# A hybrid encoder layer on one core: outputs of attention and of the delta rule handed on in fp32, split by the merge, and the first delta tile joined from 16-row blocks

## What is computed

```
ya = oa.reshape(b, t, WIDTH_A) @ w['w_branch_a']      # oa: attention over the selected keys
yb = ob @ w['w_branch_b']                             # ob: gated delta rule, normed and gated
merged = jax.nn.sigmoid(gate_a) * ya + jax.nn.sigmoid(gate_b) * yb
x = x + merged @ w['w_out']
```

```
sol = lax.linalg.triangular_solve(a, rhs, left_side=True, lower=True, unit_diagonal=True)
v_new = u - w @ state
new_state = state * exp(g_last) + k_faded @ v_new
```

## Time and profile before

| | us |
|---|---|
| median of three runs (lowest, highest) | 3028.71 (3026.67, 3028.89) |
| the profiled execution, its own time | 3023.2 |
| its span in the profile | 3021.4 |
| attend ends, first DMA of delta | 1702.39 |
| first DMA of merge | 1940.39 |
| first product with w_out in merge | 1990.40 |

### The profile page before, as it was taken

One profiled execution on the slowest core, in us unless ns is written; L12 is line 12 of the kernel. 1 busy time (PEld: TensorE's weight loads), 2 busy tenths in 40 slices (PEclk: granted clock), 3 DMA queues, 4 the chain that ended last, 5 costly groups with the idle time before them and its releaser, 6 DMA issues. The chain is left out here.

```text
span 3021.4 us, 43869 instructions
## 1 busy us (share of the span) xinstructions
PE 2860.3 (95%) x16073; PEld 2681.7 (89%) x16073; DVE 1655.0 (55%) x2958; ACT 848.2 (28%) x1485; POOL 373.0 (12%) x470
## 2 busy tenths in 40 slices
PE   6999999999989999999889788699899999999998
PEld 6999999999989789999878688588789999999997
DVE  5444444444451378899355467467744444444445
ACT  4111111111132434554276334211221111111112
POOL 0000000000000034444230266210000000000000
PEclk9999999999999999999989799899999999999999
DMA  4111111111022112222210323732121111111111
GB/s 135 53 43 42 42 42 42 42 42 42 8 53 47 29 53 89 82 89 89 75 53 20 88 68 98 222 124 82 42 64 42 42 42 42 42 42 42 42 35 63
DMA packets 248861, 183.55 MB, mean 61 GB/s; under 512 B 46329, under 2 KB 230185, under 8 KB 248754
## 3 DMA queue, kind: packets, MB, share of 16 engines
q1 hardware_dynamic: 241602, 153.74, 17.6%
q10 hardware_dynamic: 4752, 18.94, 1.7%
q0 software_dynamic: 2400, 9.44, 0.9%
HBM read 142.37 MB, written 39.65 MB: 60 GB/s over the span
## 5 line engine op out<-in xcount | busy, mean ns | idle before, releaser
L506 DVE TENSOR_TENSOR ffn_prod<-ffn_silu,ffn_p_up 128x384 f32<-128x384 f32 x132 | 73.2, 554 | 768.7 <-ACT ffn_silu L426 768.7
L488 DVE SCALAR_TENSOR_TENSOR x<-ffn_p_down,x 128x512 f32<-128x512 f32 x738 | 474.9, 687 | 1.3 <-PE ffn_p_down L157 1.3
L157 PE MATMUL ffn_p_gate<-ffn_hT_hi,ffn_g_hi 128*128 128x384 f32 x1056 | 356.7, 338 | 17.9 <-ACT ffn_silu L426 10.8
L157 PE MATMUL ffn_p_gate<-ffn_hT_lo,ffn_g_hi 128*128 128x384 f32 x1056 | 355.3, 336 | 0.0
L157 PE MATMUL ffn_p_gate<-ffn_hT_hi,ffn_g_lo 128*128 128x384 f32 x1056 | 355.1, 336 | 0.0
L157 PE MATMUL ffn_p_up<-ffn_hT_hi,ffn_u_hi 128*128 128x384 f32 x1056 | 353.8, 335 | 0.0
L157 PE MATMUL ffn_p_up<-ffn_hT_hi,ffn_u_lo 128*128 128x384 f32 x1056 | 353.2, 334 | 0.0
L157 PE MATMUL ffn_p_up<-ffn_hT_lo,ffn_u_hi 128*128 128x384 f32 x1056 | 353.0, 334 | 0.0
L426 ACT ACTIVATE ffn_silu<-ffn_p_gate 128x384 f32<-128x384 f32 x132 | 64.9, 492 | 870.5 <-PE ffn_p_up L157 870.4
L157 PE MATMUL ffn_p_down<-o_c_hi,o_t_lo 128*128 128x512 f32 x756 | 295.4, 391 | 0.0
L157 PE MATMUL ffn_p_down<-o_c_lo,o_t_hi 128*128 128x512 f32 x756 | 295.0, 390 | 0.0
(11 more groups left out here) (390 smaller groups left out, 5137.8 us busy)
## 6 DMA issues: line engine op xcount, KB each, us to landing
ffn_raw_g<-in_ffn_w_gate SPq DMA_DIRECT2D x44, 512.0 KB, 5.1
ffn_raw_u<-in_ffn_w_up SPq DMA_DIRECT2D x44, 512.0 KB, 6.2
ffn_raw_d<-in_ffn_w_down SPq DMA_DIRECT2D x44, 512.0 KB, 3.6
h_raw<-in_w_in SPq DMA_DIRECT2D x32, 512.0 KB, 3.9
projected_d<-sp_stage ACTq DMA_DIRECT2D x20, 576.0 KB, 2.8
conv_d<-sp_stage ACTq DMA_DIRECT2D x12, 576.0 KB, 3.2
dl_qkv<-conv_d SPq DMA_DIRECT2D x27, 256.0 KB, 4.1
x<-in_x_prompt SPq DMA_DIRECT2D x8, 512.0 KB, 8.3
```

Of the source, the lines that this page charges most:

```text
L157: mm = nc.tensor.matmul(out, stationary(k)[a], moving(k)[b], start=(start and at == 0 and i == 0), stop=(stop and 3 * at + i == n - 1))
L488: nc.vector.scalar_tensor_tensor(out=xs, in0=p_down[(NO * q + o) % 4][:], scalar=0.5, in1=xs, op0=ALU.mult, op1=ALU.add).then_inc(added, 1)
L506: nc.vector.tensor_tensor(prod[:, slot], silu[:, slot], p_up[slot][:, 0:TG], ALU.mult).then_inc(prod_done, 1)
```

## The change

Three things. (1) `attend` writes its turned output once, unsplit, from two alternating buffers (`oT[:, t % 2]`), and the sample units once, from a buffer of their own; DVE's `keep_rest` and `keep_rest_dec` go, `turn_out_dec` follows three units behind instead of four. (2) `delta` writes the gated output unsplit and straight from the gate's buffer, for tiles 3 to 8; tiles 0 to 2 (the merge's first third) are split by `keep_high` and `keep_rest` into SBUF operands that stay there. The attended output of the first third is loaded raw at step 5 and split in step 7. A gate buffer of tile 5 or later is reloaded only when the store out of it has landed, and the stage's end waits for those stores. The merge loads raw thirds, casts on ACT and subtracts on DVE, with one raw buffer for a and, for b, the second half of `gate_a` and part of `gate_b`'s; the third third is loaded when the second has been split. (3) Tile 0 is solved on POOL like the others, so its step has three levels; fronts of tiles 0 and 1 are both made ahead of step 0. `take_log` moves ahead of `keep_high`, `sum_squares` of the last two tiles ahead of the state products of the sample tile, and the constant planes shrink from ten to three.

```diff
@@ attend @@
-            for t in range(NTP):
-                sp.wait_ge(oT_rest, t + 1)
-                for i in range(2):
-                    sp.dma_start(a_parts_d[i][...], oT[:, i].bitcast(F32)).then_inc(stored, 16)
+            for t in range(NTP):
+                sp.wait_ge(oT_ready, t + 1)
+                sp.dma_start(attended_d[...], oT[:, t % 2]).then_inc(stored[t % 2], 16)
+            sp.wait_ge(oT_ready, NTP + 2)
+            sp.dma_start(attended_d[...], oT_dec[:]).then_inc(stored_dec, 16)
...
@@ delta, SP @@
             def load_gate(n):
-                if n >= 2:
+                if 2 <= n < 2 + FIRST:
                     sp.wait_ge(lo_done, n - 1)
+                elif n >= 2:
+                    sp.wait_ge(gated_stored, 16 * (n - 1 - FIRST))
...
             def store(n):
-                sp.wait_ge(lo_done, n + 1)
-                for i in range(2):
-                    sp.dma_start(b_parts_d[i][...], parts[:, i].bitcast(F32)).then_inc(parts_stored, 16)
+                sp.wait_ge(normed, n + 1)
+                sp.dma_start(gated_d[...], gate[:, n % 2]).then_inc(gated_stored, 16)
...
             load(2)
-            to_blocks(1)
             sp.dma_start(gain[:], ...)
             load_gate(0)
             load_gate(1)
+            send_lower(0)
+            to_blocks(0)
+            send_lower(1)
+            from_blocks(0)
+            to_blocks(1)
             for n in range(NT):
...
                 if n + 1 < NT:
                     from_blocks(n + 1)
                 if n + 2 < NT:
+                    send_lower(n + 2)
                     to_blocks(n + 2)
+                if n >= 3 + FIRST:
+                    store(n - 3)
                 if n >= 3:
-                    store(n - 3)
                     load_gate(n - 1)
-                if n == NTP - 2:
-                    first.load(sp, a_parts_d, b_parts_d)
+                if n == NTP - 3:
+                    first.load(sp, attended_d)
...
+            sp.wait_ge(gated_stored, 16 * (NT - FIRST))
@@ delta, PE @@
-            rows_and_k(0)
-            q_and_v(0)
-            turn_hats(0)
-            grams_k(0)
-            grams_q(0)
-            turn_first()
+            for m in range(2):
+                rows_and_k(m)
+                q_and_v(m)
+                turn_hats(m)
+                grams_k(m)
+                grams_q(m)
@@ delta, ACT and DVE @@
-                    if n >= 3 and third == 2:
-                        keep_high(n - 3)
+                    if n == NTP - 1 and third == 0:
+                        first.keep_high_a(act)
                     if n >= 2 and third == 2:
                         take_log(n - 2)
+                    if 3 <= n < 3 + FIRST and third == 2:
+                        keep_high(n - 3)
...
+                    elif n == NTP - 1 and third == 0:
+                        first.keep_rest_a(dve)
...
-                if n >= 3:
-                    keep_rest(n - 3)
+                    if 3 <= n < 3 + FIRST and third == 2:
+                        keep_rest(n - 3)
@@ delta, POOL @@
             front(0)
-            for m in range(1, NT):
+            front(1)
+            solve(0)
+            solve(1)
+            for m in range(2, NT):
                 front(m)
                 solve(m)
@@ merge @@
+            for g in range(1, NG):
+                if g >= 2:
+                    sp.wait_ge(a_rest, g - 1)
+                sp.dma_start(raw_a[:], attended_d[...]).then_inc(raw_a_in, 16)
+                if g >= 2:
+                    sp.wait_ge(b_rest, 2 * (g - 1))
+                for i in range(2):
+                    sp.dma_start(raw_b[i], gated_d[...]).then_inc(raw_b_in, 16)
             weights.load_out(sp, 0)
             weights.load_branches(sp, 1)
...
             weights.branches_hi(act, 0)
-            weights.out_hi(act, 0)
-            weights.branches_hi(act, 1)
             for n in range(KD):
                 for g in range(NG):
+                    if n == 0 and g + 1 < NG:
+                        split_high(g + 1)
+                    if n == 0 and g == 1:
+                        weights.out_hi(act, 0)
+                        weights.branches_hi(act, 1)
                     act.wait_ge(summed, NG * n + g + 1)
...
+                    if n == 0 and g + 1 < NG:
+                        split_rest(g + 1)
...
+                    if n == 0 and g:
+                        pe.wait_ge(a_rest, g)
...
+                    if n == 0 and g:
+                        pe.wait_ge(b_rest, 2 * g)
```

More of the change, by code:

```diff
@@ L2134, in _ @@
             for h in range(HB):
+                if h < 2:
+                    sum_squares(NTP - 1 + h)
                 pe.wait_ge(v_spread, h + 1)
@@ L2264, in keep_rest @@
                 dve.wait_ge(hi_done, n + 1)
[L2265 to L2268 removed]
+                tokens = slice(n * P, (n + 1) * P)
+                nc.vector.tensor_tensor(first.b_lo[:, :, tokens], gate[:, n % 2], first.b_hi[:, :, tokens].bitcast(F32),
+                                        ALU.subtract).then_inc(lo_done, 1)
             def next_state(n):
@@ L2436, in keep_high @@
                 act.wait_ge(normed, n + 1)
-                if n:
-                    act.wait_ge(parts_stored, 32 * n)
-                nc.scalar.copy(parts[:, 0], gate[:, n % 2]).then_inc(hi_done, 1)
+                nc.scalar.copy(first.b_hi[:, :, n * P:(n + 1) * P], gate[:, n % 2]).then_inc(hi_done, 1)
             def step(n):
@@ L2628, in __init__, with load, keep_high_a, keep_rest_a @@
     def __init__(self, nc, s):
-        self.parts = [[s.sbuf(f"{n}_{part}", [P, HB, TG], F32R) for part in ("hi", "lo")] for n in ("a", "b")]
-        self.outputs = s.sbuf("outputs", [P, 2, HB, P], F32R)
-        self.operands_in, self.parts_stored = s.sem("operands_in"), s.sem("parts_stored")
-    def load(self, sp, *parts_d):
-        sp.wait_ge(self.parts_stored, 32 * (TG // P))
-        load_operands(sp, self.parts, parts_d, slice(0, TG), self.operands_in)
-def load_operands(sp, parts, parts_d, tokens, landed):
-    for part, part_d in zip(parts, parts_d):
-        for i in range(2):
-            sp.dma_start(part[i][:].bitcast(F32), part_d[i][:, :, tokens].rearrange("n p t -> p n t")).then_inc(landed, 16)
-def merge(nc, x, weights, ops, first, parts_d, projected_d):
+        self.nc = nc
+        self.a_hi, self.a_lo, self.b_hi, self.b_lo = (s.sbuf(n, [P, HB, TG], F32R) for n in ("a_hi", "a_lo", "b_hi", "b_lo"))
+        self.raw = s.sbuf("raw", [P, HB, TG])
+        self.raw_in, self.high, self.rest = s.sem("raw_in"), s.sem("high"), s.sem("rest")
+    def load(self, sp, attended_d):
+        sp.dma_start(self.raw[:], attended_d[:, :, 0:TG].rearrange("n p t -> p n t")).then_inc(self.raw_in, 16)
+    def keep_high_a(self, act):
+        act.wait_ge(self.raw_in, 16)
+        self.nc.scalar.copy(self.a_hi[:], self.raw[:]).then_inc(self.high, 1)
+    def keep_rest_a(self, dve):
+        dve.wait_ge(self.high, 1)
+        self.nc.vector.tensor_tensor(self.a_lo[:], self.raw[:], self.a_hi[:].bitcast(F32), ALU.subtract).then_inc(self.rest, 1)
+def merge(nc, x, weights, ops, first, attended_d, gated_d, projected_d):
     KB = HB
```

315 lines of the change are left out of this document (126 added, 189 removed).

## The result

Five executions of the changed kernel took 3003.05 to 3013.57 us, median 3009.31; five of the kernel before 3024.92 to 3028.89, median 3026.67. The ratio is 0.9941, with a 95% interval of 0.9926 to 0.9955: faster by 17.4 us, half as much again as the 11.8 forecast, and inside the range by 1.3 us at its lower end (3008). The profiled execution, 3003.05, is the quickest of the five, so its profile shows 20.1 less than that of before, not 17.4. "Delta" is from its first DMA to the merge's first DMA, "merge's start" from there to the first product with `w_out`.

A forecast was written before the change was run, and what follows sets the result against it. PE bounds the untouched feed-forward stages; attend's end, delta (solve loop first, then DVE and PE handing over) and the merge's first 50 us can move. -2.4 + 4.7 - 3.0 - 4.3 - 6.8 = -11.8, so 3016.9 us; range 3008 to 3026.

The forecast's parts named there:

- Attend, -2.4: End of attend: last units no longer wait for high part, rest and store in turn; -2.4 us, bounds -0.6 to -3.4.
- Delta's start, +4.7: Start of delta: solve 1 starts 5.9 us later, 1.2 won back; +4.7, bounds +3.5 and +7.5.
- the solve's loop: In delta: solve, writes, packed reads, next solve; a period of 20.2 us, to which the steps may shrink.
- Delta's steps, -3.0: Steps of delta: earlier `take_log` -1.9, two rests gone -1.3 and -0.7, step 7's added work +0.9; -3.0 us, bounds -5 and 0.
- 0.48 a step: Steps 3 to 6 of delta: PE's wait that goes with `take_log` ahead of `keep_high`; -1.9 us in all.
- the 3.6 of the estimate: Step 7 of delta: the 128x1536 subtraction beside solve 8 grows from 1.85 to 3.6 us, making the steps' sum 1.8 worse.
- Delta's end, -4.3: End of delta: last store follows the norm -4.2, its landing +2.3, one store less -0.4, earlier norm -2.0; bounds -6 and -1.
- one of the signs of being wrong: Tail of delta: the prediction is wrong if gate loads stall POOL there.
- Merge, -6.8: Start of the merge: cast of `w_out` at 18.4 us against 25.3, so `out` starts 6.8 sooner; bounds -9.5 and +4.5.
- delta's solves don't bind all the way: Rival in delta: nine solves stay the bound, start costs 7.5, steps give nothing; -6.0 us, 3022.7; 15%.
- a third's round of load and split in the merge: Rival: if it takes over 12 us rather than 8, the merge gains nothing; -5.0 us, 3023.7; 15%.
- solve 0 was not late: Rival in delta: solve 0 starts only at 1739.5, start costs 20.2, steps give nothing; +6.7 us, 3035.4; 6%.

The follow-up runs named there:

- again: The changed kernel once more, unchanged, timed and profiled a second time: 3007.21 us, 0.9936 of the kernel before.
- six_levels: The changed kernel without its third part: tile 0 joined from 2-row blocks in six levels again, not solved on POOL; 3003.78 us, 0.9926 of the kernel before.
- all_rests: The changed kernel with cast and subtraction also for tiles 3 and 4, in steps 6 and 7, into an unread buffer: 3008.92 us, 0.9945 of the kernel before.
- before_order: The kernel before with one edit alone, `take_log` ahead of `keep_high` in delta's steps: 3020.67 us, 0.9982 of the kernel before.
- order: The changed kernel with `take_log` behind `keep_high` again, in steps 3 to 5: 3010.70 us, 0.9950 of the kernel before.
- both: The changed kernel with tile 0 in six levels, slice 2's weights split later, and the merge's loads in one row: 3000.67 us, 0.9915 of the kernel before.
- late_gates: The changed kernel with slice 2's two gate loads in the merge held back until slice 1's first product is gated: 3005.43 us, 0.9937 of the kernel before.

## Why the prediction was right, and where it was not

In short: the total lies in the range and each part moved the way that was said, but delta's steps gave more than twice what was said, and by a mechanism that the prediction had priced too low: two instructions in the wrong order on ACT delay PE, and through PE they bring DVE's subtraction behind POOL's scaling.

**What bounds.** The three stages and no other moved by the change: from the first product with `w_out` to the merge's last the three profiles agree within 0.1, and the 2.1 by which "again" is longer lie behind the merge.

**Attend, -2.4.** Right. The wait I counted at 1.3 is 1.3 shorter (2.12 to 0.82), and attend is 2.0 shorter in "again". The 4.8 of the first profile holds 2.75 more, which the clock accounts for (see "again").

**Delta's start, +4.7.** The place was right, the size wrong. Step 1 started 2.6 to 3.8 late, not 5.9, and 1.1 to 3.4 of it was won back by expansion 4, not 1.2 of 5.9. I had taken the solve's loop as fixed at 20.2. That was a mean: in before, solves start 19.35 to 20.91 apart, and here solve 1 starts 15.9 after solve 0. That solve 0 starts within 0.3 of the forecast is luck: I had POOL decide it, which was free 4.3 sooner than I said, and SP did, 0.9 later than I said (its terms as listed add up to 1725.9, not to 1726.3). Of the 1.6 of waits that I took to be the second period's, 0.44 stand at the last expansion of before. Net, at expansion 4: +0.4 to +1.5 against before, -0.4 to +0.8 against six_levels; over all seven profiles with the solve of tile 0 it is +0.4 to +3.8 against before, and the whole delta is 0.1 to 3.6 longer with it than in the kernel that differs by it alone.

**Delta's steps, -3.0.** This is the step that failed, by a mis-sized term: -7.0. I priced the order of `take_log` by the wait in PE's row, 0.48 a step (in step 3 it is 0.89), and the two rests apart. The runs show 1.4 to 1.8 a step for the order (5.0 in three), because the wait also pushed the subtraction behind POOL's scaling. The fourth period lost 2.35, of which all_rests gives the cast and the rest 0.4 and before_order the order 1.04; what remains of it is open. And the steps shrank to 19.46, below the solve's 20.2 that I had set as their limit.

**The rule on DVE and POOL.** I read the 1.36 of the subtraction as "while POOL was solving". The rows say otherwise: it is 1.36 where POOL's scaling of the queries (1.27, 128x512) began first, and 0.68 where the subtraction began 0.02 ahead, and then POOL's took 1.79. The 128x1536 subtraction beside solve 8 took 1.75, not the 3.6 of the estimate: POOL's solve is made of many short instructions, and it paid for the overlap itself: one of its instructions, begun 0.17 behind the subtraction, took 1.74 instead of 0.29 and so ended 0.16 after it (the whole solve took 11.0 from its start to the transposed copy, where the two solves before took 10.0). The Trainium skill, page "SBUF — State Buffer", section "Who interferes with whom", says that a DVE instruction with two SBUF inputs contends with a GpSimd instruction that reads SBUF, that what they share is an exclusive lock, and that issue order decides who blocks: the trace agrees, with 0.68 and 1.79 in the one order, 1.36 and 1.28 in the other. My estimate used the rule without asking how long each single instruction of POOL is, and which of the two would begin first.

**Delta's end, -4.3.** -3.6. The last store follows the norm as said, but the norm no longer ends the list; the last new state does, 1.2 later. From the end of the last store's issue, landing and barrier took 5.1, with three stores issued within 2.9; I had counted 2.3 for the landing, on top of what stood there before (2.47 from the last subtraction's end, two issues and the barrier). The gate's reload behind a landing did make POOL wait 2.23 for the sample tile, one of the signs of being wrong that I had named; DVE, working on the new states, did not wait for it. The clock has a part in the tails: before, six_levels and order have no stretch at 0.50 in the first 30 us of theirs, and there the gain is 4.1 (40.37 to 36.2); the six profiles with one of 3.4, some 18 in, stand at 36.8 to 36.9, and both, with 6.8, at 38.53.

**Merge, -6.8.** Right in mechanism and nearly in size: -5.2. The cast of `w_out` and POOL's end came within 0.3 of the forecast. What I took as "the list of before" took 20.0 instead of 18.1: the second of slice 2's weights was cast 9.5 behind its issue instead of 8.0. Four gate loads were issued around it in both kernels, in the change all within 1.6, before within 2.2 with a wait ahead of the third. late_gates takes two of them away and gets 1.5 to 1.7 back, so the gates' share in that time is shown; why it grew from before to after is not.

**Sum and rivals.** With the measured terms: -2.0 + (0.4 to 1.5) - 7.0 - 3.6 - 5.2 = -17.4 to -16.3, against -17.4 of the medians. The closeness is luck: the terms are taken from two executions, whose spans are 20.1 and 14.1 shorter than before's. The two largest misses, delta's steps and its start, both made the change look smaller than it is. No rival took place: delta's solves don't bind all the way, a third's round of load and split in the merge took at most 8.5 and not over 12, and solve 0 was not late.

Left open: what remains of the fourth period's 2.35, and why slice 2's weights were cast later than before. That single subtractions in attend were free was not tried by itself.

## What to carry to other kernels

The price of a wait is not its own length: look at what the delayed instruction meets next. Here 0.5 to 0.9 of PE's wait made a DVE instruction arrive behind a POOL instruction instead of ahead, and the step lost two to three times as much. Order first what another engine waits for, and put the copies that only a later stage needs behind it: two lines that changed places took 3.6 us from delta in the kernel before. And when loads shrink, check the next transfer in the row: part of the merge's gain went to gates that were asked for long before they were needed.

## What was not expected of the hardware

Two engines' instructions decide by some 20 ns which of them waits: DVE at 1812.25 and POOL at 1812.27 took 0.68 and 1.79; DVE at 1854.90 behind POOL at 1854.88 took 1.56 instead of 0.69. Such a collision, set off by data that came 0.77 late, made the period 2 to 3 of delta 20.3 in one execution where it was 18.9 in another of the same kernel. And PE's wait of 6.74 in the merge cost more than itself: the granted clock fell from 1.00 to 0.50 at 1961.3, while PE stood, and rose again at 1968.2; the first 12 products behind it took 3.97, starting 0.32 apart, where at full clock they start 0.17 apart.
